# Feed-forward output tiles in pairs over four PSUM banks in a two-block, two-layer fp32 model

## The chip, the cores and the metric

The kernel runs on one core of a Trainium2 chip. The metric is device microseconds of one execution, the median over the runs. Lower is better.

## What is computed

A sequence of 512 rows with 1024 features goes through an attention layer and a pooling layer (the first block), and then through two transformer layers `l = 0` and `l = 1` (the second block). The part that the change touches is the feed-forward half of these two layers:

```
h = rmsnorm_2(x, mlp_norm[l])
u = jnp.square(jax.nn.relu(jnp.einsum('bsd,df->bsf', h, w_ff1[l])))   # 1024 -> 4096
x = x + jnp.einsum('bsf,fd->bsd', u, w_ff2[l])                        # 4096 -> 1024
```

After `l = 1` the result is `rmsnorm_2(x, final_norm)`.

## The kernel before

Everything lies transposed, with features on the partitions: `xT` is 8 tiles (`kt`) of 128 features by 512 positions. A full-precision product is made of three fp32r matmuls. Each weight tile is split by ScalarE into a high part `WH` (a copy, L486) and by VectorE into a low part `WL` (raw minus high, L748). Both are one call of `conv(t)`, once on each engine, for tile number `t`. Activations are split in the same way into `MH`/`ML` and `XH`/`XL`. `three` (L1204) issues `WL·xh`, `WH·xl` and `WH·xh` into one PSUM bank (L1206, L1207, L1208).

The 4096 hidden features are taken in `BLOCKS = 4` blocks of 1024. In each block `ff_block` has 16 output tiles of 128x512, each with 8 values of `k`, so 24 matmuls. Tiles `i < 8` are the first product: they read `MH`/`ML`, VectorE takes the relu out of PSUM into `tb` (L1159), ScalarE squares it into `sq` and `XH` (L703, L704), VectorE makes `XL` from them (L1163). Tiles `i >= 8` are the second product: they read `XH`/`XL`, and VectorE adds the result to `xT` (L954). In the last block of a layer ScalarE also makes the next `MH` (L494) and the square (L500), GpSimd sums the squares into `acc` (L457), and VectorE makes the next `ML` (L754).

The order on each engine is written out by hand and tied by counting semaphores:

- Weights have four slots, `t % 4`. `conv(t)` waits for `psum_done` of the tile that used the slot last, `t - 4`. In iteration `i` each of ScalarE and VectorE first does `conv(t0 + i + 2)` and then the work on result `i`. TensorE waits for `lo_done >= t + 1` before tile `t`.
- Results have two banks, `U[:, r % 2]`. TensorE's `begin(r)` waits until VectorE has taken result `r - 2` (`result_taken >= r - 1`).
- `raw` holds two loads of 1 MB from HBM, each of which is two weight tiles. A load into one half waits until both tiles that were there are converted.
- After the first tile of a layer's feed-forward half comes `stat` (L1276, L1279 on TensorE): the mean square by two kinds of matmul into `Z`, then ScalarE's logarithm and exponential (L507, L508), and VectorE's three steps to `rstd` (L763, L764, L766). VectorE does this ahead of result 0, since L1159 multiplies by `rstd`.

After the last tile of `l = 0` TensorE goes on to the first projection tile of `l = 1` (`dfk`, again by `three`, into `U`). After that of `l = 1` it transposes half of the output (`y_turn`, L1520), then computes the last row statistics from `acc` (L1532) and the last square (L1533).

Of the kernel before, what the change touches and what calls it, by code (L numbers as in the profile page):

```python
# [12 lines left out]
P = 128  # L13
# [102 lines left out]
def build(nc, x, norm_g, attn_w_in, attn_sinks, attn_w_out, pool_w_in, pool_w_mix, pool_scale,  # L116
# [3 lines left out]
    KT = D // P  # L120
# [3 lines left out]
    BLOCKS = FF // D  # L124
    plan = make_plan(DEPTH)
    LAST_T = plan["tiles"]
# [11 lines left out]
    with ExitStack() as ctx:  # L138
# [9 lines left out]
        XH, XL = sb("XH", [P, KT, S], F32R), sb("XL", [P, KT, S], F32R)  # L148
        MH, ML = sb("MH", [P, KT, S], F32R), sb("ML", [P, KT, S], F32R)
# [144 lines left out]
        def y_bank(m):  # L294

            return [PP[:, 0, :], PP[:, 1, :], O[:], Z[:, 0:512], Z[:, 1024:1536], U[:, 0, :], U[:, 1, :], PP[:, 0, :]][m]

        def rev(ap, z0, z1):
            return ap[:, z0:z1][:, ::-1]
# [162 lines left out]
        def _(act):  # L462
# [11 lines left out]
            def conv(t, loop=None):  # L474

                if loop is None:
                    if t >= LAST_T:
                        return
                    act.wait_ge(raw_landed[t // 2 % 2], 16 * (t // 4 + 1))
                    if t >= 4:  # L480
                        act.wait_ge(psum_done, freed[t - 4])
                else:
                    act.wait_ge(raw_landed[t // 2 % 2], loop * 64 + 16 * (t // 4 + 1))
                    act.wait_ge(psum_done, loop * 16 + (loop_r[0] + t - 3))
                src, shape = raw_view(t)
                a.activation(w_slot(WH, t, shape), src, ACT.Copy).then_inc(hi_done, 1)  # L486
# [186 lines left out]
            for l in range(DEPTH):  # L673
                for s in plan["layer", l]:
                    t, j = s["t"], s["j"]
                    layer_begin(s, l)
                    layer_end(s, l)
                    if s["kind"] in ("dfk", "dfq"):

                        act.wait_ge(psum_done, s["r"] + 1)  # L680
                        act.wait_ge(result_taken, s["r"])
                        for q in range(4):
                            o = q ^ 1
                            i = a.activation(tb[32 * q:32 * q + 32, 0, :], U[32 * o:32 * o + 32, s["r"] % 2, :], ACT.Copy)
                        i.then_inc(rope_shifted, 1)
                    for st in s["steps"]:
                        if st["op"] == "stat":
                            stat(st)
                    if s["kind"] == "wo" and s["second"]:
                        for i in range(2):  # L690
                            prep(G_MLP + 8 * l, 2 * (j - 4) + i, s["r"] + i, dst=MH)
                t0, r0 = plan["ff", l]
                loop_r[0] = r0 - t0

                def ff_block(b, first=False, last=False):
                    for i in range(16):
                        if t0 + 16 * (BLOCKS - 1) + i + 2 < LAST_T or not last:
                            conv(t0 + i + 2, b)
                        if first and i == 0:
                            stat(plan["ff_stat", l])  # L700
                        if i < 8:
                            act.wait_ge(result_taken, b * 16 + (r0 + i + 1))
                            a.activation(sq[:, i % 2, :], tb[:, i % 2, :], ACT.Square).then_inc(relu_squared, 1)  # L703
                            a.activation(XH[:, i, :], tb[:, i % 2, :], ACT.Square).then_inc(second_hi_ready, 1)  # L704
                        elif last:

                            prep(G_ATTN + 8 * (l + 1) if l < DEPTH - 1 else None, i - 8, r0 + 16 * b + i, dst=MH)

                ff_block(0, first=True)
                with act.Fori(1, BLOCKS - 1) as b:  # L710
                    ff_block(b)
                ff_block(BLOCKS - 1, last=True)
# [9 lines left out]
        def _(dve):  # L722
# [365 lines left out]
            for l in range(DEPTH):  # L1088
# [60 lines left out]

                def ff_block(b, first=False, last=False):  # L1150
                    for i in range(16):
                        if t0 + 16 * (BLOCKS - 1) + i + 2 < LAST_T or not last:
                            conv(t0 + i + 2, b)
                        if first and i == 0:
                            stat(plan["ff_stat", l])
                        ps = result(r0 + i, b)
                        if i < 8:

                            v.scalar_tensor_tensor(out=tb[:, i % 2, :], in0=ps, scalar=0.0, in1=rstd[:, 0:S], op0=ALU.max,  # L1159
                                                   op1=ALU.mult).then_inc(result_taken, 1)  # L1160
                            dve.wait_ge(relu_squared, b * 8 + (u0 + i + 1))
                            dve.wait_ge(second_hi_ready, b * 8 + (m0 + i + 1))
                            v.tensor_tensor(XL[:, i, :], sq[:, i % 2, :], XH[:, i, :].bitcast(F32), ALU.subtract).then_inc(second_ready, 1)  # L1163
                        else:
                            kt = i - 8
                            add_x(ps, kt, last, r0 + 16 * b + i if last else None)
                            if last and l < DEPTH - 1:
                                prep_lo(G_ATTN + 8 * (l + 1), kt, (MH, ML))
                            elif last:
                                v.tensor_scalar(xf[:, kt, :], xT[:, kt, :], gain[:, G_LAST + kt:G_LAST + kt + 1], None, ALU.mult).then_inc(xt_ready, 1)  # L1170
# [16 lines left out]
        def _(pe):  # L1187
# [273 lines left out]
            for l in range(DEPTH):  # L1461
# [29 lines left out]
                m_seen += 8  # L1491
                t0, r0 = plan["ff", l]

                def ff_block(b, first=False):
                    for i in range(16):
                        t, r = t0 + i, r0 + i
                        pe.wait_ge(lo_done, b * 16 + (t + 1))
                        o = begin(r, b)
                        for k in range(KT):
                            if first and i == 0:  # L1500
                                pe.wait_ge(normed_ready, 24 + 16 * l + k + 1)
                            if i == 8:
                                pe.wait_ge(second_ready, b * 8 + (m_seen + k + 1))
                            h_, l_ = (MH, ML) if i < 8 else (XH, XL)
                            c = slice(P * k, P * k + P)
                            last = three(o, WH[:, t % 4, c], WL[:, t % 4, c], h_[:, k, :], l_[:, k, :], k == 0, k == KT - 1)
                        last.then_inc(psum_done, 1)
                        if first and i == 0:
                            stat(plan["ff_stat", l])

# [12 lines left out]
            st = plan["last_stat"]  # L1523
            pe.wait_ge(z_free, st["z"])
            pe.wait_ge(o_free, plan["o"])
            for m in range(NB):
                y_turn(m)
            pe.wait_ge(acc_done, sum(sums))
# [42 lines left out]
```

## Time and profile before

| | |
|---|---|
| time, median of 3 runs | 1695.18 us (1694.88 to 1695.56) |
| span of the profiled execution | 1694.2 us |
| TensorE (PE) busy, share of the span | 1640.7 us, 97% |
| VectorE (DVE) busy | 936.5 us, 55% |
| ScalarE (ACT) busy | 708.1 us, 42% |
| feed-forward of `l = 0` from its second tile on | 702.4 to 1050.6 us, with the first tile of the next layer |
| feed-forward of `l = 1` from its second tile on | 1338.4 to 1681.4 us |

The profile's time for that execution is its span, from the first to the last instruction; what lies around it is not shown, and the median of the timed runs is 1.0 us above the span. A TensorE matmul's record is longer than the distance to the next one, since matmuls overlap. The distance between two starts is what one costs.

### The profile page before, as it was taken

What the parts mean: (1) busy time and instruction counts of PE and PEld (TensorE: products, weight loads), DVE (VectorE), ACT (ScalarE), POOL (GpSimd) and SP (SyncE); (2) the same over time, 40 slices, a digit from 0 to 9 for tenths busy, and PEclk for the clock granted to TensorE, in tenths of its full rate; (3) what the DMA queues carried; (4) which work ended last, traced back from release to release, by engine and by line L of the source; (5) the groups of instructions that cost most, each with busy time, mean ns of one, the idle gap of its engine ahead of it and who ended that gap; (6) DMA issues with size and microseconds to landing.
All of it is one profiled execution on the core that took longest, in us unless ns stands there. A gap on an engine that the chain in (4) does not pass through costs nothing.

```text
span 1694.2 us, 20851 instructions
## 1 busy us (share of the span) xinstructions
PE 1640.7 (97%) x7745; PEld 1308.7 (77%) x7745; DVE 936.5 (55%) x1583; ACT 708.1 (42%) x1268; POOL 139.1 (8%) x131
## 2 busy tenths in 40 slices
PE   6999999999989999999999999999999999999998
PEld 4877788877778566888888888777666888888886
DVE  6566556666666766643434345575766643434343
ACT  4255543455453654432323244553664532323232
POOL 3000122023500000300000001000000200000001
PEclk9999999999999999999999999999999999999999
DMA  4201133323211211232333332211111232333331
GB/s 138 93 26 51 50 100 100 100 87 100 75 51 50 63 38 50 89 111 88 100 99 99 99 99 75 87 63 50 51 49 50 75 106 94 100 99 99 99 99 50
DMA packets 127272, 135.62 MB, mean 80 GB/s; under 512 B 2443, under 2 KB 120789, under 8 KB 127189
## 3 DMA queue, kind: packets, MB, share of 16 engines
q1 hardware_dynamic: 126084, 133.19, 24.4%
q8 instruction: 50, 0.82, 0.2%
q0 software_dynamic: 288, 1.05, 0.2%
q10 hardware_dynamic: 816, 0.30, 0.1%
q14 instruction: 34, 0.27, 0.0%
HBM read 132.43 MB, written 2.10 MB: 79 GB/s over the span
## 4 chain that ended last, share of the span: by engine, by line
PE 80%; DVE 10%; ACT 5%; issue 4%; DMA 1%; POOL 1%; SPq 0%; DVEq 0%; POOLq 0%; ACTq 0%
PE U L1206 22%; PE U L1208 21%; PE U L1207 21%; DVE cc L890 3%; PE Z L1393 3%; PE O L1447 2%; PE Z L1305 2%; DVE ea L892 2%; PE O L1331 2%; DVE ea L887 1%; PE U L1249 1%; PE U L1250 1%; PE U L1251 1%; PE O L1441 1%; DMA raw<-in_attn_w_in 1%
## 5 line engine op out<-in xcount | busy, mean ns | idle before, releaser
L1206 PE MATMUL U<-XH,WL 128*128 128x512 f32 x976 | 385.2, 395 | 3.9 <-issue 3.4
L1208 PE MATMUL U<-XH,WH 128*128 128x512 f32 x976 | 381.2, 391 | 0.0
L1207 PE MATMUL U<-XL,WH 128*128 128x512 f32 x976 | 381.0, 390 | 0.0
L748 DVE TENSOR_TENSOR WL<-raw,WH 128x1024 fp32r<-128x1024 f32 x246 | 313.7, 1275 | 58.0 <-ACT WH L486 53.5
L486 ACT ACTIVATE WH<-raw 128x1024 fp32r<-128x1024 f32 x246 | 257.0, 1049 | 209.5 <-PE U L1208 173.6
L1206 PE MATMUL U<-MH,WL 128*128 128x512 f32 x848 | 335.7, 396 | 1.9 <-DVE tb L1075 1.7
L1208 PE MATMUL U<-MH,WH 128*128 128x512 f32 x848 | 330.8, 390 | 0.0
L1207 PE MATMUL U<-ML,WH 128*128 128x512 f32 x848 | 330.2, 389 | 0.0
L1206 PEld LDWEIGHTS U<-XH,WL 128*128 128x128 f32 x976 | 184.0, 189 | 43.4 <-issue 5.6
L1208 PEld LDWEIGHTS U<-XH,WH 128*128 128x128 f32 x976 | 183.8, 188 | 38.9
L1207 PEld LDWEIGHTS U<-XL,WH 128*128 128x128 f32 x976 | 184.1, 189 | 36.9
L954 DVE TENSOR_TENSOR xT<-xT,U 128x512 f32<-128x512 f32 x112 | 76.8, 686 | 206.7 <-PE U L1208 205.0
L1206 PEld LDWEIGHTS U<-MH,WL 128*128 128x128 f32 x848 | 159.3, 188 | 40.2 <-issue 5.3
L1208 PEld LDWEIGHTS U<-MH,WH 128*128 128x128 f32 x848 | 159.2, 188 | 33.8
L1207 PEld LDWEIGHTS U<-ML,WH 128*128 128x128 f32 x848 | 159.4, 188 | 31.3
L703 ACT ACTIVATE sq<-tb 128x512 f32<-128x512 f32 x64 | 40.4, 631 | 249.2 <-DVE tb L1159 249.2
L454 POOL TENSOR_SCALAR acc<-sq 128x512 f32<-128x512 f32 x7 | 11.3, 1608 | 1118.6 <-ACT sq L500 1118.6
L1159 DVE SCALAR_TENSOR_TENSOR tb<-U,rstd 128x512 f32<-128x512 f32 x64 | 44.2, 691 | 89.4 <-PE U L1208 89.3
L1393 PE MATMUL Z<-keys,queries 64*128 64x512 f32 (+3 forms) x256 | 90.2, 462 | 0.0
L1163 DVE TENSOR_TENSOR XL<-sq,XH 128x512 fp32r<-128x512 f32 x64 | 44.3, 692 | 80.6 <-ACT XH L704 80.6
L1249 PE MATMUL U<-WL,MH 128*128 128x256 f32 x256 | 76.2, 298 | 8.8 <-DVE queries L1113 5.8
L457 POOL TENSOR_TENSOR acc<-acc,sq 128x512 f32<-128x512 f32 x48 | 69.2, 1442 | 122.6 <-ACT sq L500 122.2
(218 smaller groups left out, 1784.7 us busy)
## 6 DMA issues: line engine op xcount, KB each, us to landing
raw<-in_w_ff SPq DMA_DIRECT2D x64, 1024.0 KB, 5.3
raw<-in_w_in SPq DMA_DIRECT2D x24, 1024.0 KB, 5.2
raw<-in_attn_w_in SPq DMA_DIRECT2D x10, 1024.0 KB, 5.2
raw<-in_pool_w_in SPq DMA_DIRECT2D x8, 1024.0 KB, 5.4
raw<-in_w_o SPq DMA_DIRECT2D x8, 1024.0 KB, 5.1
raw<-in_attn_w_out SPq DMA_DIRECT2D x4, 1024.0 KB, 5.2
raw<-in_pool_w_out SPq DMA_DIRECT2D x4, 1024.0 KB, 5.1
xin<-in_x SPq DMA_DIRECT2D x2, 1024.0 KB, 8.5
```

The costliest lines, as they stand in the source:

```text
L457: g.tensor_tensor(dst[:], dst[:], sq[:, n % 2, :], ALU.add).then_inc(acc_done, 1)
L486: a.activation(w_slot(WH, t, shape), src, ACT.Copy).then_inc(hi_done, 1)
L748: v.tensor_tensor(w_slot(WL, t, shape), src, w_slot(WH, t, shape).bitcast(F32), ALU.subtract).then_inc(lo_done, 1)
L890: i = v.tensor_tensor_scan(rev(cc, z0, z1), ones[:].to_broadcast([P, z1 - z0]), rev(ea[:, 0, :], z0, z1), 0.0, ALU.mult, ALU.add)
L954: i = v.tensor_tensor(xT[:, kt, :], xT[:, kt, :], ps, ALU.add)
L1159: v.scalar_tensor_tensor(out=tb[:, i % 2, :], in0=ps, scalar=0.0, in1=rstd[:, 0:S], op0=ALU.max, op1=ALU.mult).then_inc(result_taken, 1)
L1163: v.tensor_tensor(XL[:, i, :], sq[:, i % 2, :], XH[:, i, :].bitcast(F32), ALU.subtract).then_inc(second_ready, 1)
L1206: mm(o, wl, xh, start=first, stop=False, **kw)
L1207: mm(o, wh, xl, start=False, stop=False, **kw)
L1208: return mm(o, wh, xh, start=False, stop=last, **kw)
L1249: mm(o2, a[:, k, q], wl, start=k == 0, stop=False)
L1393: i = mm(Z[:, z0:z0 + w], qk[name + "q"][rows_, j, P * n:P * n + P], qk[name + "k"][rows_, j, 0:w], start=True, stop=True)
```

## The change

`ff_bank(i)` gives the result of feed-forward tile `i` one of four banks: `PP[0]`, `PP[1]`, `U[0]`, `U[1]`, in turn. The `PP` banks serve transposes elsewhere. TensorE now works on two tiles at a time, in `ff_pair`: for each `k` it issues the six matmuls of both. In `l = 0` they alternate between the two banks by matmul, with each streamed activation tile used twice in a row. In `l = 1` a tile's three matmuls of one `k` stand together, in the order `WL·xh`, `WH·xh`, `WH·xl`. Both tiles' `psum_done` come at the pair's end. ScalarE and VectorE convert two weight tiles together in every even iteration.

```
+        def ff_bank(i):
+            return PP[:, i % 2, :] if i % 4 < 2 else U[:, i % 2, :]
...
                 def ff_block(b, first=False, last=False):
                     for i in range(16):
-                        if t0 + 16 * (BLOCKS - 1) + i + 2 < LAST_T or not last:
-                            conv(t0 + i + 2, b)
+                        for n in (i + 2, i + 3) if i % 2 == 0 else ():
+                            if t0 + 16 * (BLOCKS - 1) + n < LAST_T or not last:
+                                conv(t0 + n, b)
...
-                        ps = result(r0 + i, b)
+                        result(r0 + i, b)
+                        ps = ff_bank(i)
...
+                def ff_pair(i, b, first):
+                    for n in (i, i + 1):
+                        pe.wait_ge(lo_done, b * 16 + (t0 + n + 1))
+                        pe.wait_ge(result_taken, b * 16 + (r0 + n - 3))
+                    o = [ff_bank(n) for n in (i, i + 1)]
+                    h_, l_ = (MH, ML) if i < 8 else (XH, XL)
+                    for k in range(KT):
...
+                        if l == 0:
+                            for n in range(2):
+                                mm(o[n], w[n], h_[:, k, :], start=k == 0, stop=False)
+                            for n in range(2):
+                                mm(o[n], h[n], l_[:, k, :], start=False, stop=False)
+                            done = [mm(o[n], h[n], h_[:, k, :], start=False, stop=k == KT - 1) for n in range(2)]
+                        else:
+                            done = []
+                            for n in range(2):
+                                mm(o[n], w[n], h_[:, k, :], start=k == 0, stop=False)
+                                mm(o[n], h[n], h_[:, k, :], start=False, stop=False)
+                                done.append(mm(o[n], h[n], l_[:, k, :], start=False, stop=k == KT - 1))
+                    for x in done:
+                        x.then_inc(psum_done, 1)
...
-                    for i in range(16):
...
-                            last = three(o, WH[:, t % 4, c], WL[:, t % 4, c], h_[:, k, :], l_[:, k, :], k == 0, k == KT - 1)
-                        last.then_inc(psum_done, 1)
+                    for i in range(0, 16, 2):
+                        ff_pair(i, b, first)
                         if first and i == 0:
                             stat(plan["ff_stat", l])
...
+            pe.wait_ge(result_taken, r0 + 16 * BLOCKS - 2)
             for m in range(NB):
                 y_turn(m)
```

**The statistics on TensorE.** The rows below are TensorE's at the end of the first work of the feed-forward half of `l = 0`, before the change: the last matmuls of tile 0, the two kinds of statistics matmul, and the first of tile 1.

```order
L1206 MATMUL U<-MH,WL 128x512
L1207 MATMUL U<-ML,WH 128x512
L1208 MATMUL U<-MH,WH 128x512
L1276 MATMUL Z<-acc,mean_w 128x512
L1279 MATMUL Z<-mean_w,acc 128x1 x4
L1206 MATMUL U<-MH,WL 128x512
```

With the change, the same place (L1517 to L1520 are `ff_pair`'s matmuls, L1283 and L1286 the statistics; x2 is one for each tile of the pair):

```order
L1517 MATMUL PP<-MH,WL 128x512 x2
L1519 MATMUL PP<-ML,WH 128x512 x2
L1520 MATMUL PP<-MH,WH 128x512 x2
L1283 MATMUL Z<-acc,mean_w 128x512
L1286 MATMUL Z<-mean_w,acc 128x1 x4
L1517 MATMUL U<-MH,WL 128x512 x2
```

The statistics have moved from behind one tile to behind two, and the next work is a pair in the `U` banks.

**VectorE behind the statistics.** Before, from the three `rstd` steps on:

```order
L763 SCALAR_TENSOR_TENSOR nt<-rstd 128x516
L764 TENSOR_TENSOR nt<-nt,Z 128x516
L766 SCALAR_TENSOR_TENSOR rstd<-nt,rstd 128x516
L1159 SCALAR_TENSOR_TENSOR tb<-U,rstd 128x512
L1163 TENSOR_TENSOR XL<-sq,XH 128x512
L748 TENSOR_TENSOR WL<-raw,WH 128x1024
L1159 SCALAR_TENSOR_TENSOR tb<-U,rstd 128x512
```

With the change, from the same place (L1166 is the relu, L1170 makes `XL`, L753 converts):

```order
L768 SCALAR_TENSOR_TENSOR nt<-rstd 128x516
L769 TENSOR_TENSOR nt<-nt,Z 128x516
L771 SCALAR_TENSOR_TENSOR rstd<-nt,rstd 128x516
L1166 SCALAR_TENSOR_TENSOR tb<-PP,rstd 128x512
L1170 TENSOR_TENSOR XL<-sq,XH 128x512
L1166 SCALAR_TENSOR_TENSOR tb<-PP,rstd 128x512
L1170 TENSOR_TENSOR XL<-sq,XH 128x512
L753 TENSOR_TENSOR WL<-raw,WH 128x1024 x2
```

Both results of a pair now stand ahead of the next conversions, and the two conversions stand together.

**TensorE from `l = 0` to `l = 1`.** Before, the end of the loop over blocks and the first projection tile, with the semaphores that it waits for:

```order
L1208 MATMUL U<-XH,WH 128x512
L1512 REGISTER_ALU
L1512 COMPARE_AND_BRANCH
L1206 MATMUL U<-MH,WL 128x512 [waits normed_ready,result_taken,lo_done]
L1207 MATMUL U<-ML,WH 128x512
```

With the change:

```order
L1520 MATMUL U<-XH,WH 128x512 x2
L1537 REGISTER_ALU
L1537 COMPARE_AND_BRANCH
L1213 MATMUL U<-MH,WL 128x512 [waits normed_ready,result_taken,lo_done]
L1214 MATMUL U<-ML,WH 128x512
```

The projection tile waits as before for the result of feed-forward tile 14, whose bank it takes over; that tile now ends beside tile 15.

## Rows read from the trace of the kernel before

**Rows 1.** The page: busy time, share of the span, instructions.

```profile
PE 1640.7 (97%) x7745; PEld 1308.7 (77%) x7745; DVE 936.5 (55%) x1583; ACT 708.1 (42%) x1268; POOL 139.1 (8%) x131
```

**Rows 2.** The page's costliest groups: count, busy us, mean ns, idle time before.

```profile
L1206 PE MATMUL U<-XH,WL 128*128 128x512 f32 x976 | 385.2, 395 | 3.9 <-issue 3.4
...
L1206 PE MATMUL U<-MH,WL 128*128 128x512 f32 x848 | 335.7, 396 | 1.9 <-DVE tb L1075 1.7
```

**Rows 3.** One stretch: us, busy of PE, PEld, DVE, ACT, POOL, clock, DMA, GB/s.

```profile
702.40:1050.60 348.20, 348.20 (x1538) 288.42 (x1538) 152.73 (x171) 111.25 (x146) 11.39 (x8) 1.00 0.30 97
```

**Rows 4.** Line L1206 in 702.4 to 1050.6 us: durations in ns, first and last start.

```profile
L1206 PE MATMUL U<-MH,WL x256: 389/389/475, 702.5 to 1050.1; 128*128 128x512 f32 x128
```

**Rows 5.** Timeline of PE where one tile ends and the next begins (start, us).

```profile
735.00 0.39 PE L1208 MATMUL U<-MH,WH 128*128 128x512 f32 x1
735.23 0.39 PE L1206 MATMUL U<-MH,WL 128*128 128x512 f32 x1
735.46 0.39 PE L1207 MATMUL U<-ML,WH 128*128 128x512 f32 x1
```

**Rows 6.** Timeline of PE in a value tile, whose weights are streamed.

```profile
437.47 0.28 PE L1249 MATMUL U<-WL,MH 128*128 128x256 f32 x1
437.59 0.28 PE L1250 MATMUL U<-WH,ML 128*128 128x256 f32 x1
437.71 0.28 PE L1251 MATMUL U<-WH,MH 128*128 128x256 f32 x1
437.83 0.28 PE L1249 MATMUL U<-WL,MH 128*128 128x256 f32 x1
```

**Rows 7.** Timeline of DVE in the feed-forward's steady state.

```profile
735.43 0.69 DVE L1159 SCALAR_TENSOR_TENSOR tb<-U,rstd 128x512 f32<-128x512 f32 x1 [1.30 <-PE U L1208]
...
746.31 0.69 DVE L954 TENSOR_TENSOR xT<-xT,U 128x512 f32<-128x512 f32 x1 [1.30 <-PE U L1208]
746.91 1.22 DVE L748 TENSOR_TENSOR WL<-raw,WH 128x1024 fp32r<-128x1024 f32 x1
```

**Rows 8.** Timeline of DVE behind the statistics of layer `l = 0`.

```profile
706.20 0.69 DVE L1159 SCALAR_TENSOR_TENSOR tb<-U,rstd 128x512 f32<-128x512 f32 x1
708.17 0.69 DVE L1163 TENSOR_TENSOR XL<-sq,XH 128x512 fp32r<-128x512 f32 x1 [1.29 <-ACT XH L704]
709.12 1.23 DVE L748 TENSOR_TENSOR WL<-raw,WH 128x1024 fp32r<-128x1024 f32 x1 [0.25 <-ACT WH L486]
710.26 0.68 DVE L1159 SCALAR_TENSOR_TENSOR tb<-U,rstd 128x512 f32<-128x512 f32 x1
```

**Rows 9.** Timeline of ACT, two conversions back to back.

```profile
742.65 1.99 ACT L486 ACTIVATE WH<-raw 128x1024 fp32r<-128x1024 f32 x2
```

**Rows 10.** Timeline of PE around the statistics of layer `l = 0`.

```profile
700.79 1.03 PE L1276 MATMUL Z<-acc,mean_w 128*128 128x512 f32 x2
...
702.46 0.47 PE L1206 MATMUL U<-MH,WL 128*128 128x512 f32 x1
702.77 0.39 PE L1207 MATMUL U<-ML,WH 128*128 128x512 f32 x1
```

**Rows 11.** Timeline of a wait of PE for a bank that DVE frees.

```profile
1072.92 0.69 DVE L1113 TENSOR_TENSOR queries<-tb,queries 128x512 f32<-128x512 f32 x1
...
1073.67 0.38 PE L1249 MATMUL U<-WL,MH 128*128 128x256 f32 x1 [1.17 <-DVE queries L1113]
```

**Rows 12.** Timelines of DVE and PE where layer `l = 0` ends.

```profile
1045.51 0.69 DVE L954 TENSOR_TENSOR xT<-xT,U 128x512 f32<-128x512 f32 x1 [0.90 <-PE U L1208]
1047.06 0.75 DVE L754 SCALAR_TENSOR_TENSOR ML<-xT,gain,MH 128x512 fp32r<-128x512 f32 x1 [0.86 <-ACT MH L494]
...
1050.76 1.02 PE L1276 MATMUL Z<-acc,mean_w 128*128 128x512 f32 x2
```

**Rows 13.** Timelines of DVE, POOL and PE at the kernel's end.

```profile
1676.13 0.69 DVE L954 TENSOR_TENSOR xT<-xT,U 128x512 f32<-128x512 f32 x1 [4.23 <-PE U L1208]
...
1677.57 1.28 POOL L457 TENSOR_TENSOR acc<-acc,sq 128x512 f32<-128x512 f32 x1 [4.16 <-ACT sq L500]
...
1681.38 1.04 PE L1520 MATMUL PP<-ident,xf 128*128 128x128 f32 x8
...
1683.13 0.31 PE L1532 MATMUL Z<-mean_w,acc 128*128 128x1 f32 x2
```

**Rows 14.** DMA issues: size and median time from issue to landing.

```profile
raw<-in_w_ff SPq DMA_DIRECT2D x64, 1024.0 KB, 5.3
```

More of the change, by code:

```diff
@@ L1151, in ff_block @@
                     for i in range(16):
-                        if t0 + 16 * (BLOCKS - 1) + i + 2 < LAST_T or not last:
-                            conv(t0 + i + 2, b)
+                        for n in (i + 2, i + 3) if i % 2 == 0 else ():
+                            if t0 + 16 * (BLOCKS - 1) + n < LAST_T or not last:
+                                conv(t0 + n, b)
                         if first and i == 0:
                             stat(plan["ff_stat", l])
-                        ps = result(r0 + i, b)
+                        result(r0 + i, b)
+                        ps = ff_bank(i)
                         if i < 8:
@@ L1492, in _ @@
                 t0, r0 = plan["ff", l]
-                def ff_block(b, first=False):
-                    for i in range(16):
[L1496 to L1505, printed above, removed]
-                            last = three(o, WH[:, t % 4, c], WL[:, t % 4, c], h_[:, k, :], l_[:, k, :], k == 0, k == KT - 1)
-                        last.then_inc(psum_done, 1)
+                def ff_pair(i, b, first):
[5 more added lines that the diff above has]
+                    for k in range(KT):
+                        if first and i == 0:
+                            pe.wait_ge(normed_ready, 24 + 16 * l + k + 1)
+                        if i == 8:
+                            pe.wait_ge(second_ready, b * 8 + (m_seen + k + 1))
+                        c = slice(P * k, P * k + P)
+                        h, w = [WH[:, (t0 + i + n) % 4, c] for n in range(2)], [WL[:, (t0 + i + n) % 4, c] for n in range(2)]
+                        if l == 0:
[12 more added lines that the diff above has]
+                        x.then_inc(psum_done, 1)
```

## The prediction

> **What bounds the kernel now.** I read the page's busy shares first: PE is busy for 97% of the span and no other engine for more than 55% [rows 1]. The costliest groups then say whether PE waits. Two groups of line L1206 stand for all 1824 first matmuls of a three, and 5.8 us of idle time stand ahead of them in the whole kernel [rows 2]. The window over the feed-forward of layer l = 0 has PE busy in every microsecond, at a granted clock of 1.00, which is 2.4 GHz [rows 3]. A busy PE need not be at its peak, so what counts is the distance of starts. Line L1206 starts 512 times from 702.5 to 1050.1 us (256 for each operand; 256 of them in this row), every third matmul: 347.6 / (511 x 3) = 0.2267 us each [rows 4]. One tile of 24 is 5.44 us, a pair 10.88 us. So the feed-forward (3072 matmuls, 696 us) is bound by that distance alone. The change can only gain by making it smaller, and loses wherever PE comes to wait.
>
> **The distance of two matmuls.** 512 columns at 2.4 GHz are 0.2133 us, so 0.0133 us more stand in each. The change sets two things beside each other that could bear on it, and the trace has both already. First, a change of bank: tiles alternate between U[0] and U[1], so the first matmul of a tile goes to another bank than the one before it. At such a seam the starts are 735.00, 735.23 and 735.46: 0.23 into the new bank and 0.23 within it [rows 5]. Second, the same streamed operand twice: in a value tile L1250 and L1251 both stream WH. Their starts are 0.12 apart, as are L1249 to L1250, where the streamed tile changes, and L1251 to L1249 [rows 6]; 256 columns are 0.1067 us, so the surplus is 0.013 us again. I take the distance to be unchanged: 0 us. The bounds are one TensorE cycle more or less, 3072 x 0.0004 = 1.3 us either way, and the first rival.
>
> A rule of the Trainium skill speaks for a gain. "Perfetto Trace Analysis", section "Matmul Optimizations", wants all PSUM banks in use for the most parallelism. "TensorE: Matmul & The Clock Gate", section "Back-to-back issue gap", gives N/2.4 + 2.5 ns for the gap, 215.7 ns measured, against 226.7 ns by this case's row. If more banks gave that gap, an estimate from the page is 3072 x 0.011 = 34 us less. By rows 5 and 6 it is 0.
>
> **The steady state.** With pairs, the weights of pair p+1 can be converted only when pair p-1 has ended, since there are four slots. At a seam T, DVE takes the first result 0.20 us later (735.43 against 735.23) [rows 5, 7]. From that relu, L1163 starts 1.97 us on [rows 8]. The next relu can follow 0.60 us later, the step from L954 to L748 [rows 7]: 2.57 us per result. From the second relu the first conversion starts 2.92 us on and the next instruction 1.14 us after that [rows 8]; ACT's two copies take 1.99 us together and so stay ahead [rows 9]. The second conversion takes 1.22 us [rows 7]. Sum from the first relu: 2.57 + 2.92 + 1.14 + 1.22 = 7.85 us; from T, 8.05 us. PE needs them at T + 10.88: 2.8 us of slack, stall 0. In the second product the results are one 0.69 us add each, so there is more slack. k = 7 of the first pair of the second product is read 42 matmuls in, 9.5 us after T, and XL[7] is there at about 0.20 + 2.57 + 1.97 + 0.69 = 5.4 us. A load takes 5.3 us [rows 14] and has a pair (10.88 us) and more. Fewer waits are issued on PE, which costs nothing now and gains nothing. All this is 0 us.
>
> **Seam one, the statistics (twice).** They now follow tile 1, and DVE has two results and two conversions behind them. Let S be the start of the statistics. PE's next work starts at S + 1.67 (702.46 - 700.79) [rows 10]. DVE's first relu starts at S + 5.41 (706.20 - 700.79) [rows 8, 10], because ACT and DVE must first make rstd. The conversions for tiles 4 and 5 are then complete at S + 5.41 + 7.85 = S + 13.26, and PE goes on 0.06 us later (1073.67 against 1072.92 + 0.69) [rows 11]. The pair that hides this (tiles 2 and 3) ends at S + 1.67 + 10.88 + 0.1 = S + 12.65; the 0.1 is what a restart costs, since the first step after one is 0.31 and not 0.23 [rows 10]. The stall is 13.32 - 12.65 = 0.67, with its own restart 0.77 us. Behind it, the next chain starts with the next pair and is covered again. Before, one result and one conversion stood there: no wait. Two layers: 1.5 us. Bounds: 0.3 to 1.3 us each (0.5 us of error in a chain of five hand-overs).
>
> **Seam two, l = 0 to l = 1.** The first projection tile goes to U[0], where tile 14 was. Before, tile 14 had been taken a tile (5.44 us) earlier. Now it ends one matmul ahead of tile 15. With T = 1050.76 - 5.44 = 1045.32, DVE's add starts 0.19 us behind the end of its tile [rows 12], so at T - 0.23 + 0.19, takes 0.69, and 0.06 us later PE goes on: T + 0.71, with the restart 0.8 us. Next to be late would be ML[7]: the first add, then 1.55 us to L754 [rows 12] and 0.75 for it, about 2.2 us for kt = 6, twice that, 4.5 us, for kt = 7, against 21 matmuls, T + 0.8 + 4.8. Covered. The squares' sum ends near T + 5.7, and the statistics start at T + 6.3. Bounds 0.6 to 1.2 us.
>
> **Seam three, the end.** Let T be 1681.38. Tile 14 of l = 1 ends three matmuls before (0.68 us), its add starts at T - 0.48. POOL's sum of its square ended 2.72 us after its add began (1677.57 + 1.28 - 1676.13): now T + 2.24, and 0.06 more. The transposes keep PE until T + 1.75, where L1532 starts now [rows 13]. So it starts 0.55 us later, and all behind it too. Bounds 0.3 to 1.0 us.
>
> Start of each feed-forward half: WL of the second tile is complete before its first tile begins, and the normed operands are now read at half the pace. 0 us.
>
> **Sum.** 1.5 + 0.8 + 0.55 = 2.9 us on the profiled span of 1694.2, that is 1697.1; the median of the runs stands 1.0 us above that span, so the time is 1695.18 + 2.9 = **1698.1 us**. By the terms' bounds 1696.7 (1.5) to 1700.0 (4.8). A measurement of this kernel tells a change of 0.2%, 3.4 us, from none, so this is just inside of no change.
>
> **The rivals.**
> - *The distance falls.* If a part of the 0.0133 us is the wait for one's own bank, l = 0 loses it at each of 1536 matmuls and l = 1 at each third: at 0.011 us, 17 + 6 = 23 us less, less the 2.9: 1675 us. It decides from 0.001 us per matmul on. For it: the surplus is there, and all threes stay in one bank. Against it: a seam with a change of bank has the same 0.23, and 512 starts make the same mean. Chance 0.08.
> - *The seams cost more than their sum.* The same three waits, each toward its upper bound: over 3.4 us, 1698.6 to 1700.5. It decides at 0.5 us beyond the sum. For it: the stall behind the statistics is a small difference of two long chains. Chance 0.22.
> - *The steady chain is too long.* If the chain of 8.05 us ran over 10.88, PE would stall at the pairs of each first product, 4 x 4 x 2 = 32 times. It decides at 2.8 us; 0.3 us beyond it is 10 us, 1708. Against it: each piece is a row. With it a distance that grows by three cycles or more (4 us, 1702). Chance 0.08 for both.
> - *The seams are hidden.* Were the statistics' wait covered and the end's too, 1695.2 to 1696.7. Chance 0.06.
>
> The forecast itself, 1696.7 to 1698.6, has 0.56.
>
> **The numbers.** Faster by over 0.2% is the first rival: 0.08. Slower by over 0.2% is the second and third: 0.30. The rest, 0.62, is within 0.2%. The range 1695.0 to 1701.5 leaves out the first rival and the far end of the third, with a part of the terms' error.
>
> **What the profile after would show.** Starts 0.2267 us apart in both layers' pairs; a shorter distance in l = 0 alone is the first rival. A wait of PE of about 0.7 us for DVE's conversion, once per layer, ahead of the pair behind tiles 2 and 3. A wait of about 0.7 us for DVE's add at the first projection tile of l = 1. The last L1532 2.3 us behind the last feed-forward matmul's successor. No wait at the other pairs. A wait at each of them, or any other mean distance, proves the prediction wrong.

## The result

| | before | changed |
|---|---|---|
| time, median of 20 runs each | 1694.70 us | 1698.38 us |
| span of the profiled execution | 1694.2 us | 1697.4 us |

The ratio is 1.002, with a 95% interval from 1.0013 to 1.0027: 2.2 to 4.6 us slower. In a second comparison (11 runs against 31, label e_after_again) it was 1.0016, interval 1.0007 to 1.0025. The forecast was 2.9 us more, 1698.1 us; the medians say 3.7 more and the spans 3.2.

The page of the changed kernel, busy time, answers to [rows 1]:

```profile
PE 1644.2 (97%) x7745; PEld 1310.4 (77%) x7745; DVE 931.0 (55%) x1583; ACT 706.2 (42%) x1268; POOL 139.4 (8%) x131
```

The three seams are in the timeline of PE of the changed kernel, one after the other. A row with x2 holds two matmuls, 0.23 us apart; its first number is the start of the first.

```profile
718.26 0.61 PE L1520 MATMUL U<-MH,WH 128*128 128x512 f32 x2
719.55 0.70 PE L1517 MATMUL PP<-MH,WL 128*128 128x512 f32 x2 [0.68 <-DVE WL L753]
...
1045.62 0.61 PE L1520 MATMUL U<-XH,WH 128*128 128x512 f32 x2
1046.83 0.47 PE L1213 MATMUL U<-MH,WL 128*128 128x512 f32 x1 [0.60 <-issue]
...
1684.04 1.04 PE L1545 MATMUL PP<-ident,xf 128*128 128x128 f32 x8
1686.31 0.38 PE L1558 MATMUL Z<-mean_w,acc 128*128 128x1 f32 x2 [0.35 <-POOL acc L461]
```

Seam one: the last matmul of the pair starts at 718.26 + 0.23 = 718.49 and the next at 719.55, which is 1.07 us by the trace's nanoseconds where 0.23 is due: 0.84 too much. Seam two: 1045.85 to 1046.83, 0.99 in the same way: 0.76 too much. The profile puts this one down to "issue", which would hide it from a reader of the waits; the VectorE rows below name it. Seam three: L1558 starts 2.27 us behind the first transpose, where it was 1.75 [rows 13]. PE has no other wait in the pairs: in its list of waits, the pairs' lines stand only with these two rows (one for each layer):

```profile
PE PP L1524 <- DVE WL L753: 0.7, 1, 0.7
PE PP L1517 <- DVE WL L753: 0.7, 1, 0.7
```

The chain behind the statistics, the timeline of DVE of the changed kernel, against [rows 8]:

```profile
711.44 0.69 DVE L1166 SCALAR_TENSOR_TENSOR tb<-PP,rstd 128x512 f32<-128x512 f32 x1
713.42 0.69 DVE L1170 TENSOR_TENSOR XL<-sq,XH 128x512 fp32r<-128x512 f32 x1 [1.29 <-ACT XH L709]
714.03 0.68 DVE L1166 SCALAR_TENSOR_TENSOR tb<-PP,rstd 128x512 f32<-128x512 f32 x1
716.00 0.69 DVE L1170 TENSOR_TENSOR XL<-sq,XH 128x512 fp32r<-128x512 f32 x1 [1.29 <-ACT XH L709]
716.93 2.36 DVE L753 TENSOR_TENSOR WL<-raw,WH 128x1024 fp32r<-128x1024 f32 x2 [0.24 <-ACT WH L490]
```

Both results, each held up 1.29 us by ACT's squares, then both conversions, complete at 719.29: 7.85 us from the first relu. PE starts at 719.55, 0.26 us later. In the steady state the same chain begins at 730.53 and is complete at 736.02 + 2.36 = 738.38, and the next pair starts at 741.43 without a wait.

Where l = 0 ends, the timeline of DVE of the changed kernel, against [rows 12]:

```profile
1046.05 0.69 DVE L959 TENSOR_TENSOR xT<-xT,U 128x512 f32<-128x512 f32 x1 [3.00 <-PE U L1520]
1047.59 0.75 DVE L759 SCALAR_TENSOR_TENSOR ML<-xT,gain,MH 128x512 fp32r<-128x512 f32 x1 [0.86 <-ACT MH L498]
```

The add out of U[0] ends at 1046.74, and PE's projection tile starts at 1046.83. The distance within the steady pairs has not moved. Timelines of PE of the changed kernel, l = 0 and l = 1, against [rows 5]:

```profile
734.63 0.62 PE L1517 MATMUL U<-MH,WL 128*128 128x512 f32 x2
735.09 0.61 PE L1519 MATMUL U<-ML,WH 128*128 128x512 f32 x2
...
1500.43 0.39 PE L1524 MATMUL U<-XH,WL 128*128 128x512 f32 x1
1500.66 0.39 PE L1525 MATMUL U<-XH,WH 128*128 128x512 f32 x1
1500.88 0.39 PE L1526 MATMUL U<-XL,WH 128*128 128x512 f32 x1
```

In l = 0 two starts take 0.46 or 0.45 us (0.2267 each), and in l = 1 one takes 0.23 or 0.22.

### The profile page after: what moved, and what is told of

Its sections match the earlier page's. It is cut to its first block, busy times and chain, and to the rows that moved or that the text cites. A ratio compares the mean times of both kernels' runs of the same rounds, so it can differ in the third digit from the quotient of the medians.

```text
span 1697.4 us, 20852 instructions
## 1 busy us (share of the span) xinstructions
PE 1644.2 (97%) x7745; PEld 1310.4 (77%) x7745; DVE 931.0 (55%) x1583; ACT 706.2 (42%) x1268; POOL 139.4 (8%) x131
## 4 chain that ended last, share of the span: by engine, by line
PE 79%; DVE 10%; ACT 5%; issue 4%; DMA 1%; POOL 1%; SPq 0%; DVEq 0%; POOLq 0%; ACTq 0%
PE U L1213 8%; PE U L1215 8%; PE U L1214 8%; PE PP L1517 3%; PE PP L1520 3%; PE PP L1524 3%; PE PP L1519 3%; PE PP L1525 3%; PE PP L1526 3%; PE U L1517 3%; PE U L1520 3%; PE U L1519 3%; PE Z L1400 3%; PE U L1525 3%; PE U L1524 3%
## 5 line engine op out<-in xcount | busy, mean ns | idle before, releaser
L753 DVE TENSOR_TENSOR WL<-raw,WH 128x1024 fp32r<-128x1024 f32 x246 | 307.8, 1272 | 44.4 <-ACT WH L490 40.1
L1213 PE MATMUL U<-XH,WL 128*128 128x512 f32 x464 | 185.9, 401 | 5.2 <-issue 4.5
L1215 PE MATMUL U<-XH,WH 128*128 128x512 f32 x464 | 182.0, 392 | 0.0
L1214 PE MATMUL U<-XL,WH 128*128 128x512 f32 x464 | 181.8, 392 | 0.0
L1213 PE MATMUL U<-MH,WL 128*128 128x512 f32 x336 | 137.1, 408 | 2.5 <-DVE tb L1080 1.7
L1215 PE MATMUL U<-MH,WH 128*128 128x512 f32 x336 | 132.0, 393 | 0.0
L1214 PE MATMUL U<-ML,WH 128*128 128x512 f32 x336 | 131.7, 392 | 0.0
L1213 PEld LDWEIGHTS U<-XH,WL 128*128 128x128 f32 x464 | 87.9, 189 | 24.7 <-issue 6.7
L1215 PEld LDWEIGHTS U<-XH,WH 128*128 128x128 f32 x464 | 87.6, 189 | 18.8
L1214 PEld LDWEIGHTS U<-XL,WH 128*128 128x128 f32 x464 | 88.0, 190 | 17.0
L1170 DVE TENSOR_TENSOR XL<-sq,XH 128x512 fp32r<-128x512 f32 x64 | 44.3, 692 | 80.2 <-ACT XH L709 80.2
L1213 PEld LDWEIGHTS U<-MH,WL 128*128 128x128 f32 x336 | 63.5, 189 | 21.4 <-issue 6.3
```

Of the source, the lines that this page charges most:

```text
L753: v.tensor_tensor(w_slot(WL, t, shape), src, w_slot(WH, t, shape).bitcast(F32), ALU.subtract).then_inc(lo_done, 1)
L1213: mm(o, wl, xh, start=first, stop=False, **kw)
L1214: mm(o, wh, xl, start=False, stop=False, **kw)
L1215: return mm(o, wh, xh, start=False, stop=last, **kw)
```

## The experiments

Medians are set against runs of the kernel before taken beside them: 1694.66 us for e_conv_first, e_end_singles, e_no_seams and e_banks_alone, 1695.15 us for e_after_again, e_end_singles_again, e_orders_swapped and e_layer_banks. The other four (e_two_banks, e_slack4, e_slack6, e_bf16) are one execution each, beside one of the kernel before of 1696.36 us.

A single span says little below 2 us, since executions differ by that much ahead of the feed-forward alone, where most of these edits touch nothing. So each trace is cut into stretches: from the start to the first matmul of the feed-forward of `l = 0`; from there to the statistics in the first projection tile of `l = 1` (it holds seams one and two); from there to the first feed-forward matmul of `l = 1` (its attention); and from there to the end (seam one again, and seam three). All in us, from the timelines of PE:

| run | start | feed-forward `l = 0` | attention `l = 1` | feed-forward `l = 1`, end |
|---|---|---|---|---|
| kernel before | 695.34 | 355.41 | 280.65 | 362.76 |
| changed kernel | 695.15 | 357.26 | 280.69 | 364.32 |
| e_after_again | 694.89 | 357.26 | 280.76 | 364.33 |
| e_conv_first | 695.57 | 356.29 | 281.97 | 363.37 |
| e_end_singles | 694.56 | 356.39 | 282.03 | 363.73 |
| e_end_singles_again | 694.36 | 356.38 | 282.37 | 363.73 |
| e_no_seams | 693.18 | 355.41 | 280.66 | 362.76 |
| e_banks_alone | 693.93 | 355.41 | 281.43 | 362.76 |
| e_orders_swapped | 695.12 | 356.81 | 281.59 | 365.19 |
| e_layer_banks | 692.46 | 355.41 | 279.33 | 362.77 |

The feed-forward stretches of one kernel repeat to 0.01 us. The changed kernel loses 1.85 us in the first and 1.56 us in the second, and nothing in between. The attention of `l = 1` is longer by 0.8 to 1.7 us in five of these traces, where no seam lies; there the granted clock fell. Windows of the changed kernel and then of e_end_singles (us, PE, PEld, DVE, ACT, POOL, clock, DMA, GB/s):

```profile
1200.00:1280.00 80.00, 74.36 (x368) 49.85 (x366) 58.04 (x90) 49.95 (x93) 0.00 (x0) 1.00 0.12 40
1200.00:1280.00 80.00, 76.10 (x364) 51.75 (x362) 56.78 (x88) 49.47 (x92) 0.00 (x0) 0.96 0.13 40
```

What brings the fall on there was not found.

**e_conv_first: seam one repaired.** In ScalarE's and VectorE's `ff_block`:

```
-                        for n in (i + 2, i + 3) if i % 2 == 0 else ():
+                        for n in (i + 2, i + 3) if i % 2 == 0 and not (first and i == 2) else ():
...
                         if first and i == 0:
                             stat(plan["ff_stat", l])
+                            for n in (4, 5):
+                                conv(t0 + n, b)
```

> The changed kernel, but in the first block of each layer both engines convert the weights of tiles 4 and 5 right behind the statistics, ahead of results 0 and 1. Seams theory: the two waits of 0.84 us for DVE's conversion (L753) behind the statistics are gone, with their restarts, and nothing else moves: 1.85 us less than the changed kernel, a span of 1695.6 us, 1.4 us above the kernel before. Rival (the loss lies in the pairing itself, spread over all matmuls): the span stays at 1697.4 us. Second rival (the wait only moves on to result 0, whose squares come 2.3 us later): a new wait of PE at a later pair of the first block.

Measured: median 1696.37 us, ratio 1.001, interval 1.0001 to 1.0019, where 1.4 us above before was expected and 1.7 came. Its span, 1697.2 us, is not the 1695.6 expected, and the stretches say why: both feed-forward stretches are shorter than the changed kernel's, by 0.97 and 0.95 us, 1.92 together where 1.85 was reckoned, but its start was 0.42 us longer and its attention of `l = 1` 1.28. Its DVE timeline has the conversions in front:

```profile
711.86 2.36 DVE L755 TENSOR_TENSOR WL<-raw,WH 128x1024 fp32r<-128x1024 f32 x2
714.14 0.68 DVE L1170 SCALAR_TENSOR_TENSOR tb<-PP,rstd 128x512 f32<-128x512 f32 x1
```

and its PE timeline passes the seam with no wait (L1524 is now the last line of a pair, L1521 the first of the next):

```profile
718.68 0.62 PE L1524 MATMUL U<-MH,WH 128*128 128x512 f32 x2
719.13 0.62 PE L1521 MATMUL PP<-MH,WL 128*128 128x512 f32 x2
```

The results are 2.3 us later than they were and no later pair waits, so the second rival falls too: the wait did not move, it went. The wait at the first projection tile of `l = 1` stayed, 0.76 us.

**e_end_singles and e_end_singles_again: seams two and three repaired.** On TensorE alone, with the last block taken out of the loop:

```
+                        if last and i == 14:
+                            ff_pair(14, b, first, 1)
+                            ff_pair(15, b, first, 1)
+                            continue
```

> The changed kernel, but TensorE works on tiles 14 and 15 of the last block of each layer one after the other, as before. Seams theory: the wait of 0.76 us for the bank at the first projection tile of l = 1 goes, with its restart 0.84, and the wait of 0.35 us for POOL at the last statistics, 0.52 with the shift behind it: 1.4 us less than the changed kernel, a span of 1696.0 us. Rival (spread over all matmuls): 1697.4 us.

> The kernel of e_end_singles again, since its trace had lost two of the four waits and its median had hardly fallen. Seams theory: 1.4 us less than the changed kernel beside it, 1.85 us above the kernel before. Rival (something that the waits do not show costs it 1.4 us more): as long as the changed kernel.

Measured: 1698.22 us, ratio 1.0018 (1.0009 to 1.0027), and again 1697.98 us, ratio 1.0015 (1.0005 to 1.0024). The trace does what the seams theory says. The first projection tile follows at once (timeline of PE of e_end_singles):

```profile
1045.28 0.39 PE L1520 MATMUL U<-XH,WH 128*128 128x512 f32 x1
1045.50 0.39 PE L1213 MATMUL U<-MH,WL 128*128 128x512 f32 x1
```

The wait for POOL is gone, and from the last feed-forward matmul to the end of the span it is 13.0 us as in the kernel before, against 13.6 in the changed kernel. The second median is only 0.4 us below the changed kernel's beside it, not 1.4. Both intervals hold the expected 1.0011, and so do not speak against it; but both medians lie above it. The stretches settle where that comes from in the traces: against the changed kernel the feed-forward stretches are shorter by 0.87 us (seam two) and 0.59 us (seam three), 1.46 where 1.4 was reckoned, in both traces. The attention of `l = 1`, which this edit does not touch, took 1.3 and 1.7 us more, at a granted clock of 0.96 between 1200 and 1280 us where the changed kernel had 1.00. The timed runs point the same way: their mean granted clock is 0.9925 and 0.9929, against 0.9937 for the changed kernel beside the second. Whether this order of work brings the fall on or chance does is open.

**e_no_seams: both repairs together.**

> Both repairs together: conversions of tiles 4 and 5 ahead of results 0 and 1, and tiles 14 and 15 of a layer's last block one after the other; the other 31 of 32 pairs of each layer, the four banks and the two orders stay. Seams theory: the sum of both, 3.2 us less than the changed kernel, so a span of 1694.2 us and no difference to the kernel before beyond 0.3 us. Rival (pairs or banks cost or gain by themselves, hidden under the seams): a difference to the kernel before that stays, of either sign; 0.0004 us per matmul would be 1.3 us.

Measured: median 1694.81 us against 1694.66, ratio 1.000, interval 0.999 to 1.0009. With 31 of 32 pairs of each layer, four banks and both orders still there, the loss is gone. By the medians nothing is left for pairs, banks or orders to cost or gain beyond 1.7 us either way. The trace says it far more sharply, and is the strongest evidence here: its span is 1692.0 us and not 1694.2 because its start was 2.2 us shorter, and all three stretches behind that are those of the kernel before to 0.01 us. So pairs, banks and orders by themselves cost nothing in 3072 matmuls.

**e_banks_alone: four banks without pairs.** In the kernel before:

```
-                        o = begin(r, b)
+                        pe.wait_ge(result_taken, b * 16 + (r - 3))
+                        o = ff_bank(i)
```

> The kernel before, one tile at a time, with the four banks in turn in place of two. Seams theory: banks alone cost and gain nothing, a span of 1694.2 us within 0.3, starts 0.2267 us apart. Rival (a later release of banks helped the kernel before somewhere): up to 1 us less. Rival (PP beside U costs): more than 0.5 us more.

Measured: median 1695.13 us, ratio 1.0001, interval 0.9992 to 1.001. Banks alone do nothing: both feed-forward stretches are those of the kernel before.

**e_two_banks: pairs without the additional banks.**

```
-            return PP[:, i % 2, :] if i % 4 < 2 else U[:, i % 2, :]
+            return U[:, i % 2, :]
...
-                        pe.wait_ge(result_taken, b * 16 + (r0 + n - 3))
+                        pe.wait_ge(result_taken, b * 16 + (r0 + n - 1))
```

> The changed kernel with its pairs over two banks (U alone), so each pair waits until both results of the last pair are taken. By rows: behind a pair of the first product DVE has taken the second result 0.2 + 2.57 + 0.69 us after the seam less the 0.23 or 0.68 us that tile i ends early, so a wait of 2.8 to 3.3 us at 30 pairs; behind a pair of the second product 1.0 to 1.4 us at 32; behind the statistics 7 us twice in place of 0.9. Sum about 95 + 40 + 12 = 147 us more than the changed kernel, a span near 1845 us at an unchanged clock. Rival: the waits pull the granted clock down and it is much longer, over 1950 us. Rival: banks beyond two are not needed, under 1720 us.

Measured: span 1900.0 us. The list of waits of PE (us in total, times, longest):

```profile
PE U L1517 <- DVE tb L1166: 54.2, 16, 7.0
PE U L1524 <- DVE tb L1166: 47.3, 16, 7.0
PE U L1517 <- DVE xT L959: 25.7, 16, 2.8
PE U L1524 <- DVE xT L959: 15.7, 16, 1.2
```

They sum to 142.9 us in 64 waits, of which 1.4 us stand in the changed kernel too; with a restart of 0.08 us each that is about 147 us more, as reckoned. The span is 203 us longer, not 147: the granted clock fell, which the expectation had as a rival with a larger number. The windows over both layers (us, PE, PEld, DVE, ACT, POOL, clock, DMA, GB/s):

```profile
702.00:1175.00 473.00, 393.51 (x1538) 311.93 (x1537) 146.74 (x170) 109.14 (x145) 11.33 (x8) 0.91 0.22 71
1475.00:1890.00 415.00, 357.71 (x1514) 285.99 (x1514) 140.92 (x163) 99.51 (x131) 9.21 (x7) 0.98 0.22 71
```

As an estimate, 473 x 0.09 + 415 x 0.02 is 51 us of clock; 147 + 51 is 198. So four banks are what makes pairs possible, and no gain by themselves.

**e_slack4 and e_slack6: the chain made longer.** On VectorE, with 4 or 6:

```
+                        for z in range(4 if i in (2, 4, 6, 8) else 0):
+                            v.tensor_tensor(ea[:, z // 2, 512 * (z % 2):512 * (z % 2) + 512], mask_df[:], mask_df[:], ALU.add)
                         for n in (i + 2, i + 3) if i % 2 == 0 else ():
```

> The changed kernel with four additional VectorE adds of 128x512 (into a tile that nobody reads then) ahead of the conversions in iterations 2, 4, 6 and 8 of every block. Chain theory: they take 4 x 0.61 = 2.44 us, of which DVE's present wait of about 0.3 us for ACT hides a part, so 2.1 us more on the chain of 8.0 us against 10.88: no wait at the 30 covered pairs, and 2.1 us more at each of the two waits behind the statistics: 4.2 us more than the changed kernel, a span near 1701.6 us. Rival (slack smaller than reckoned): waits at all 32, 1710 us and more.

> The same with six adds: 3.66 us, less 0.3 hidden, on the chain, 0.5 us over the slack of 2.8. Chain theory: a wait of 0.5 us, 0.6 with its restart, at 30 pairs (17 us) and 3.3 us more at the two behind the statistics (6.7 us): 24 us more than the changed kernel, a span near 1721 us. Rival (VectorE's busy time does not reach TensorE): under 1705 us. Rival (the chain was already full): over 1750 us.

Measured: spans 1704.7 and 1712.4 us, where 1701.6 and 1721 were expected. With four adds no covered pair waits, as reckoned. The waits behind the statistics grew as reckoned: the wait for L753 from 0.68 to 2.76, 2.08 us. What came on top is the clock. After the longer wait matmuls of the l = 0 pairs start 0.427 us apart; windows of e_slack4 around it:

```profile
718.00:722.00 4.00, 1.24 (x6) 0.74 (x5) 3.96 (x5) 0.00 (x1) 0.00 (x0) 1.00 0.01 2
722.00:726.00 4.00, 4.00 (x13) 3.13 (x12) 1.46 (x3) 2.57 (x5) 0.00 (x0) 0.59 0.82 255
726.00:730.00 4.00, 4.00 (x19) 3.34 (x18) 4.00 (x7) 1.63 (x2) 0.00 (x0) 0.98 0.03 11
```

4 x 0.41 + 4 x 0.02 is 1.7 us, once in each layer, 3.4 with the 4.2 of the waits: 7.6, and 7.3 were measured. The expectation had no term for the clock. With six adds the two waits grew by 3.30 us each, as reckoned, but the covered pairs hardly waited. The timeline of DVE of e_slack6 shows one chain:

```profile
800.52 0.69 DVE L1168 SCALAR_TENSOR_TENSOR tb<-PP,rstd 128x512 f32<-128x512 f32 x1 [7.12 <-PE PP L1522]
...
805.56 3.69 DVE L1158 TENSOR_TENSOR ea<-mask_df 128x512 f32<-128x512 f32 x6
809.17 2.35 DVE L753 TENSOR_TENSOR WL<-raw,WH 128x1024 fp32r<-128x1024 f32 x2
811.44 0.69 DVE L1168 SCALAR_TENSOR_TENSOR tb<-U,rstd 128x512 f32<-128x512 f32 x1
```

From relu to relu it is 10.92 us, within 0.04 of PE's 10.88, and 11.0 to the end of the conversions where 7.85 + 3.36 = 11.2 had been reckoned: DVE's adds took in more of its own waits, and each step from relu to L1172 was 0.06 us quicker. The reckoning also set the first relu 0.2 us behind the seam. Here it is at 800.52 and the next pair was due at 789.67 + 10.88 = 800.55, because the first tile of a pair ends one matmul (0.23 us) ahead of it in `l = 0`, and three (0.68 us) in `l = 1`. These two leave about 0.1 us of the 0.5. So covered pairs were late by up to 0.45 us in `l = 0`, at two to four of the four seams of a block that have the adds, and in `l = 1` by up to 0.14 us and at fewer. Why some were late by more than 0.1 us was not worked out. So 15.0 us came where 24 were expected: 6.6 in the two waits, about 5 (an estimate) in the lower clock behind them, 0.57 from 722 to 726 us and from 1367 to 1375, and the rest in the covered pairs. The direction is as reckoned: up to about 11 us of chain cost nothing, and VectorE reaches TensorE from there.

**e_bf16: what the 0.0133 us belong to.** All operands of the pairs read as bf16:

```
+                def hb(a, *at):
+                    c = at[-1]
+                    return a[:].bitcast(BF16)[(slice(None), at[0], slice(2 * c.start + 1, 2 * c.stop, 2))]
```

> The changed kernel with the operands of all 3072 feed-forward matmuls read as bf16, the high halves of the same fp32r words with a step of two, so it leaves out the lower bits of the products; number, order, banks and columns of the matmuls stay. If the surplus of 0.0133 us over 512 columns at 2.4 GHz belongs to fp32r, the starts come 0.216 us apart or less, 3072 x 0.011 = 33 us less than the changed kernel, near 1664 us. If it belongs to the change of weights or of bank whatever the type, the starts stay at 0.2267 us and the span at 1697 us.

Measured: span 1692.2 us. Its statistics of `l = 0` start at 703.35 us, 2.7 us ahead of the changed kernel's 706.03, which leaves 2.5 us for the pairs behind them, far from 33. The timelines of PE, l = 0 and then l = 1:

```profile
900.02 0.61 PE L1525 MATMUL PP<-MH,WH 128*128 128x512 bf16 x2
900.47 0.61 PE L1522 MATMUL U<-MH,WL 128*128 128x512 bf16 x2
900.92 0.61 PE L1524 MATMUL U<-ML,WH 128*128 128x512 bf16 x2
...
1500.64 0.39 PE L1529 MATMUL U<-XH,WL 128*128 128x512 bf16 x1
1500.87 0.39 PE L1530 MATMUL U<-XH,WH 128*128 128x512 bf16 x1
1501.10 0.39 PE L1531 MATMUL U<-XL,WH 128*128 128x512 bf16 x1
```

Starts are 0.225 us apart in `l = 0` and 0.227 in `l = 1`, and 1536 x 0.0017 is 2.6 us, all of the gain. The surplus over 512 columns is not the type's: nearly all of it stays. Which of the two it is, the change of weights at each matmul or a fixed cost of each matmul in this stream, no run here tells.

**e_after_again: the changed kernel beside the last runs.**

> The changed kernel once more, beside the others of this call: the yardstick for them. By its trace it loses 0.92 + 0.93 us behind the statistics, 0.84 us at the first projection tile of l = 1 and 0.6 us at the end: 3.3 us above the kernel before.

Measured: 1698.38 us, ratio 1.0016, and the same three seams in its trace (1.07, 0.99 and 1.07 us).

**e_orders_swapped: the orders exchanged.**

```
-                        if l == 0:
+                        if l == 1:
                             for n in range(2):
                                 mm(o[n], w[n], h_[:, k, :], start=k == 0, stop=False)
```

> The changed kernel with the two layers' orders exchanged: banks alternate by three matmuls in l = 0 and by matmul in l = 1. Seams theory: the order sets only how far ahead of the pair's end tile 14 ends. In l = 0 it ends 0.68 us ahead and not 0.23, so the wait at the first projection tile falls from 0.76 to 0.31 us; in l = 1 it ends 0.23 us ahead, so the last statistics come 0.45 us later. Starts stay 0.2267 us apart and the sum is that of the changed kernel within 0.1 us. Rival (alternating by matmul costs or gains per matmul): a distance of starts that differs between the layers and has changed places.

Measured: median 1698.09 us against 1698.38 for the changed kernel beside it, ratios to before 1.0019 (1.001 to 1.0028) and 1.0016. The timeline of PE where l = 0 ends, and at the kernel's end:

```profile
1045.83 0.39 PE L1526 MATMUL U<-XL,WH 128*128 128x512 f32 x1
1046.36 0.47 PE L1213 MATMUL U<-MH,WL 128*128 128x512 f32 x1
...
1687.18 0.27 PE L1558 MATMUL Z<-mean_w,acc 128*128 128x1 f32 x1 [0.81 <-POOL acc L461]
```

Seam two fell from 0.76 to 0.30 us, and the wait for POOL grew from 0.35 to 0.81: both as reckoned, 0.45 us in exchange. The last stretch is longer by 0.4 us more than that: from the last statistics to the end it took 11.5 us and not 11.1, at a granted clock of 0.58 between 1687.5 and 1694 us where the changed kernel had 0.74. So, that apart, the order of the matmuls matters in fp32r only through the moment at which tile 14 ends.

**e_layer_banks: the banks where a wait was for a bank.** On top of e_no_seams:

```
+        def res_bank(r):
+            for l in range(DEPTH):
+                rb = plan["layer", l][0]["r"]
+                if rb <= r < rb + 8:
+                    return ff_bank(r - rb)
+            return U[:, r % 2, :]
```

with TensorE's wait at these results for `result_taken >= r - 3` in place of `r - 1`.

> The kernel of e_no_seams with the four banks in turn also for the first eight results of each transformer layer's projections (k, q and v of the first half of the differential heads), in whose slots PP serves nothing else. In the kernel before PE waits there once per layer for VectorE to free a bank (1.33 us beyond the matmul's own 0.12, at 432.4 and 1073.7 us). If that wait is for the bank alone, it goes in both layers: 2.6 us less than e_no_seams, a span 2.6 us below that of the kernel before at an equal start. Rival (the weights or the next results are late by as much): the wait moves to a later tile and the time stays.

Measured: median 1691.4 us against 1695.15, ratio 0.9978, interval 0.9968 to 0.9988: 3.8 us faster than the kernel before and 7 us faster than the changed one. The tile of [rows 11], which waited 1.17 us there, in the timeline of PE of this kernel:

```profile
1072.22 0.28 PE L1270 MATMUL PP<-WH,MH 128*128 128x256 f32 x1
1072.34 0.28 PE L1268 MATMUL U<-WL,MH 128*128 128x256 f32 x1
```

0.12 us apart, no wait. Its list of waits has 3.5 us for `queries` in two places where the kernel before has 5.8 in four. Its attention of `l = 1` took 279.33 us, 1.33 less than that of e_no_seams, as reckoned for one layer. The waits account for 2.7 us with restarts; the median says 3.8, and the interval holds both. Its nine runs had a mean granted clock of 0.9967 and the kernel before 0.9947, which may be the rest; no run here separates it.

## Why the prediction was right

- **What bounds it, the distance of starts**, was right: 0.2267 us before and after, in both orders. The argument by the tile seam [rows 5] and by the value tile [rows 6] held, and the first rival fell: e_no_seams and e_banks_alone show that four banks leave the distance alone. The estimate by the Trainium skill ("TensorE: Matmul & The Clock Gate", "Back-to-back issue gap": 34 us less) did not come. That section gives its formula as the gap of a single, isolated matmul, which this stream is not, and ties it to no bank. By the Trainium skill, "Perfetto Trace Analysis", "Matmul Optimizations", all banks should be in use; here more of them paid only in e_layer_banks, where PE had waited for one.
- **Seam one** was reckoned at 0.77 us each. Measured: 0.84 in the wait and 0.08 in the restart, 0.92 in both layers (0.97 and 0.95 by the repair). The chain of 7.85 us came out to the hundredth. The term was 0.15 us short, because PE went on 0.26 us after the conversion, and not 0.06 as in [rows 11]. In `ff_pair` one more wait instruction stands behind the one for the second tile's weights, which may be what takes the rest; no run here tested it.
- **Seam two**: 0.8 reckoned, 0.76 and 0.08 measured (0.87 by the repair).
- **Seam three**: 0.55 reckoned, 0.52 measured, and 0.07 more behind it, where the next step to ACT took 1.98 us and not 1.91 (0.59 by the repair).
- **The steady state** was right: no wait in the changed kernel, none with four adds more, short ones with six (e_slack4, e_slack6). The slack was 3.05 us (738.38 to 741.43) and not 2.8, since the first tile of a pair ends ahead of the pair.
- **Sum**: 0.92 + 0.92 + 0.84 + 0.52 + 0.07 is 3.3 us, against 2.9 forecast; the two feed-forward stretches say 3.4 and the spans 3.2. The mechanism was right in all its parts, and the one term that was too small by more than 0.1 us is seam one. The measured 1698.38 us lies inside the forecast's own 1696.7 to 1698.6, partly by luck: the kernel before measured 1694.70 us beside it and not 1695.18. As a difference the medians say 3.7, beyond the bound of 0.2% at which the forecast drew its line, with an interval on both sides of it; so the second rival, the same seams toward their upper bounds, is as good a name for what came as the forecast itself. The 0.4 us between the seams and the medians are not accounted for by any run.
- That the loss lies in these seams and not in the pairing is shown by e_no_seams, whose stretches are those of the kernel before, and for each seam alone by the stretches of e_conv_first and e_end_singles. The median of e_end_singles did not resolve it.

## What to carry to other kernels

Where TensorE already starts its matmuls back to back and never waits for a bank, more banks and another order of the same matmuls bought nothing here; look for the seam between two tiles in the trace, which shows a change of bank for free. Grouping tiles makes the group's work come due at once: reckon the chain behind the group at each place where something else stands in it (statistics, the next layer, the end), because the steady state's slack says nothing of those. Spend additional banks where the list of waits names a bank. And compare traces stretch by stretch: spans that differ by 2 us for other reasons held stretches that agree to 0.01 us, and a repair of 1.5 us that the medians hid.

## What was not expected of the hardware

- With bf16 operands, starts were 0.225 us apart when banks alternate by matmul and each streamed tile comes twice, and 0.227 when they alternate by three; with fp32r both orders gave 0.2267. The cause stays open.
- A wait of 2.8 us of TensorE was followed by a fall of the granted clock from 1.00 to 0.59 over 4 us, 1.7 us of time; waits of 0.7 us were followed by none. In e_two_banks, where PE waits for some 3 us every 11 to 14, the clock's mean was 0.91 in l = 0 and 0.98 in l = 1. So a wait of that length can cost more than itself.
- In the attention of `l = 1`, where TensorE's longest wait is 1.8 us, the granted clock fell in five of the table's ten traces, and these took 0.8 to 1.7 us longer there; both traces of the changed kernel and that of the kernel before have no such fall. The cause stays open.
- Two waits for a bank that VectorE frees can stand under different names: the profile gave one to DVE [rows 11] and the one at seam two to "issue".
